# Even layer: where the modulation vectors of the experts are computed, through which slots their weights come, and when the first expert's gate is loaded

## The chip, the cores and the metric

One NeuronCore of a Trainium2 chip runs the kernel. Its engines, TensorE (PE in the rows), VectorE (DVE), ScalarE (ACT), GpSimd (POOL) and SyncE (SP, which here only issues DMAs), run their own instruction streams and meet at semaphores. The metric is the device time in microseconds of one execution.

## What is computed

A first block (gated linear recurrence beside dilated attention) makes `x` of 512 rows by 1024. Then come two layers over 512 latent and 256 context rows, the even one with a differential and a grouped attention, the odd one with a latent attention, each followed by a mixture of 16 experts. Each layer is steered by six modulation vectors, made from the condition by one wide matrix. The part that matters here is the even layer:

```python
m = silu(c) @ w_ada + b_ada          # six vectors: m[0] .. m[5], for latent and for context rows
h = modulate(rmsnorm(x), m[0], m[1])
oa = diff_attend(qa, ka, va, lam)    # the attention "ea" of the kernel
ob = gqa_attend(qb, kb, vb)          # the attention "eb"
x = x + m[2] * (concat(oa, ob) @ w_out)
h = modulate(rmsnorm(x), m[3], m[4])
aff = softmax(h @ w_router)          # then top-k tokens for each of 16 experts
y[e] = (silu(xs @ w_gate[e]) * (xs @ w_up[e])) @ w_down[e]
x = x + m[5] * scatter_add(gates * y)
```

## The kernel before

Each engine's program is written out by hand, in functions named by engine and stage (`pe_moe`, `dve_moe`, `act_norm`). An engine takes its instructions in that order, so what is written later waits behind what is written earlier.

**Weights.** SP loads all weights in one long list, `LOADS` (from line 290). Each entry has a key and a slot of 16 KB per partition; a slot is free for its next load when the matmuls of its last one are done (`slot_freed`, line 326). Slots 0 and 1 serve the projections (`two`), the experts of layer 0 cycle through `eight`. SP waits in order: a load that must wait holds up all behind it. Further waits of single loads are in `sync` (line 2882).

**Modulation vectors.** Vector j of layer l comes in two halves of 512 columns, keys `("ada", l, j, h)`, 2 MB each. `pe_ada_mm` (line 417) multiplies a half by 8 matmuls with a 32-column stationary operand, at four column positions of the array; the trace counts each matmul of this type twice. `dve_ada_row` (448) takes the result out of PSUM into a row (`row_mem`, 400). Then `pe_ada_end` (430) transposes the row into columns (j = 3, 4) or spreads it over partitions by a matmul (j = 2, 5), and `dve_ada_end` (467) puts it where it is used.

**Attentions.** `ea` (object `ATA`, line 1840) and `eb` (`ATB`, 1856) each run 48 units of 128 queries: units 0 to 31 look at 768 keys, units 32 to 47 at 256. In step s TensorE makes the scores of unit s, turns the probabilities of unit s-2 and multiplies by the values those of unit s-3. In `ea` two units are joined before the turn, so only odd units are turned. Both objects have a list of fills: extra pieces of work that each engine does when unit s-4 is through. `ea` has four small ones (copies of keys, `act_khl`, `dve_khl`), `eb` has norm pieces for VectorE and ScalarE; TensorE has none in both. The first block's attention has fills of modulation work, two matmuls at a time, from `fine` (1464).

**From attention to experts.** Behind `eb` comes the output projection (12 groups of 8 matmuls, `pe_outproj`), then `pe_moe(0)` and `dve_moe(0)`: the matmuls of vectors 3 and 4, the norm (`dve_norm`, `act_norm`), transposes and scaling (`pe_hT`, `dve_hT`), routing, top-k on VectorE, the matmuls of vector 5 under it, the indices, and the gathers of each expert's 96 rows from `h_rows` in DRAM by GpSimd. `sp_moe` (2381) writes `h_rows` and `x_rows`; it is called ahead of the second half of the first "up". The loads of vectors 3 and 4 wait for the end of `eb`, the first gate waits for the end of the output projection.

**Experts of layer 0** (`pe_experts0`): for each, gate, up and down in halves, with line 2106 for latent and 2119 for context rows.

Of the kernel before, what the change touches and what calls it, by code (L numbers as in the profile page):

```python
# [153 lines left out]
def program(nc, T, out, known):  # L154
    ctx = ExitStack()
    with ctx:
# [8 lines left out]
        AR = arena.__enter__()  # L165
# [98 lines left out]

        two, eight, ten = [0, 1], [0, 1, 2, 3, 6, 9, 4, 5], [4, 5, 0, 1, 3, 11, 9, 6, 2, 10]

# [6 lines left out]
        def expert_load(nm, l, e):  # L273
            for h in range(2):
                if (nm, l, e, h) == ("up", 0, 0, 1):
                    ada_loads(0, [5], [4, 5])
                if (nm, l, e, h) == ("gate", 1, 1, 0):
                    ada_loads(1, [5], [6, 2])
                src = T[f"w_exp_{nm}_2"][l, e, h * 512:h * 512 + 512, :]
                if (nm, l) == ("down", 0):  # L280
                    src = src.rearrange("(s p c) n -> p s (c n)", s=2, c=2)
                else:
                    src = src.rearrange("(p c) n -> p (c n)", c=4)
                cyc((nm, l, e, h), src, (4, 1024), ten if l else eight)
# [16 lines left out]
        for i, (a, b) in enumerate(EVEN_CH):  # L301
            colchunk(("even", i), T["w_in_even_2"][0], a, b, two)
        for i in range(2):
            colchunk(("oute", i), T["w_out_even_2"][0], i * 512, i * 512 + 512, two)
        ada_loads(0, [3], [8, 7])
        ada_loads(0, [4], [4, 5])
        expert_loads(0)
# [79 lines left out]
        def ada_groups(l, j):  # L387
            if l < 0:
                return [(0, 0, 128)]
            if j == 2:  # L390
                return [(1, 0, 128), (2, 1, 128)] if l == 0 else [(2, 0, 128)]
            return [(3, 0, 128), (4, 1, 128)] if l == 0 else [(3, 0, 128)]

# [6 lines left out]
        def row_mem(l, j):  # L400
            return AR[:, H0:H0 + 1024] if j == 4 else RB1

# [45 lines left out]
        def dve_ada_row(l, j, h):  # L448
            n = ADA_NO[(l, j)]
            if j == 4:  # L450
# [72 lines left out]
        def act_norm(tag):  # L523
            src, xn, nt = NORM[tag][0:3]
            for j in range(nt):
                junk = xn[:, j, :]
                if tag in ("m0", "m1"):
                    junk = AR[:, H0 + 5120:H0 + 6144]
                    S.wait_ge("res", MLAST[NORM[tag][4]], OUTP[MLAST[NORM[tag][4]]] + j)
                    if j:  # L530
                        S.wait_ge("sq", tag, j - 1)
                if tag == "no":
                    S.wait_ge(f"xr{j}", 0)
                if tag == "n1":
                    S.wait_ge(f"dx{j}", 0)
                s.activation(junk, src[:, j, :], ACT.Square, accum_out=SSQ[tag][:, j:j + 1])\
                    .then_inc(*S.up("sq", tag, j))
            act_rstd(tag)
            S.wait_ge("rs", tag)
            if tag == "m0":  # L540
                S.wait_ge("full", "ada", 0, 3, 0)
            for j in range(1, nt, 2):
                s.activation(xn[:, j, :], src[:, j, :], ACT.Copy, scale=RS[tag][1][:, j:j + 1])\
                    .then_inc(*S.up("xn_a", tag, j))
# [910 lines left out]
        units = []  # L1455
# [383 lines left out]

        ATA = Attn("ea", units, Pb4, PTb, fills={8 + 8 * i: [i] for i in range(4)})  # L1840
        units = []
        for j in range(6):
            k0, nk = (0, 768) if j < 4 else (512, 256)
            for h in range(8):
                r = h % 2
                def kready(e):
# [8 lines left out]
                                  out=OT[:, 4 + h // 2, 128 * j:128 * j + 128]))  # L1855
        ATB = Attn("eb", units, Pb4, [AR[:, H0 + 3072:H0 + 4096], GB[0], GB[3]], Rb=RbA,
                   fill=[("sq", j) for j in range(6)] + [("rstd",)] + [("mul", j) for j in range(6)])
        ssA, gsc = st(24), st(1)
# [3 lines left out]
        def pe_fillB(it):  # L1862
            pass

# [11 lines left out]
        def dve_fillB(it):  # L1876
# [5 lines left out]
            if it[0] == "rstd":  # L1882
                V.wait_ge("sub", 5)
                dve_rstd_a("sub", ssA, 1.0 / 128)
                dve_rstd_b("sub")
            if it[0] == "mul":
                j = it[1]
# [459 lines left out]
        def dve_moe(l):  # L2347
            tag = f"m{l}"
            for h in range(2):
                dve_ada_row(l, 3, h)  # L2350

            def fourth():
                for h in range(2):
                    dve_ada_row(l, 4, h)

            dve_norm(tag, fourth)
            dve_ada_end(l, 3)
            dve_ada_end(l, 4)
            dve_hT(tag)
            dve_topk(l)  # L2360
            dve_idx(l)
            dve_ada_row(l, 5, 0)
            dve_ada_row(l, 5, 1)
            dve_ada_end(l, 5)
            dve_experts1() if l else dve_experts0()

        def pe_moe(l):
            for j, b0 in ((3, 6), (4, 4)):
                for h in range(2):
                    pe_ada_mm(l, j, h, b0 + h)  # L2370
            pe_ada_end(l, 3, 6, 7)
            pe_ada_end(l, 4, 0, 1)
            pe_route(l)
            pe_topk(l)
            for h in range(2):
                pe_ada_mm(l, 5, h, 4 + h)
            pe_idx(l)
# [354 lines left out]
        def tensor():  # L2732
# [21 lines left out]
            pe_even()  # L2754
            pe_attn(ATA, lambda i: None)
            pe_pairs(ATB, pe_fillB)
# [13 lines left out]
        def vector():  # L2770
# [28 lines left out]
            V.wait_ge("full", "hturn", *HTS[-1])  # L2799
            dve_attn(ATA, dve_khl)  # L2800
            V.wait_ge("full", "pv", "ea", 47)
# [17 lines left out]
        def scalar():  # L2819
# [24 lines left out]
            S.wait_ge("full", "even", 4, 5)  # L2844
            act_attn(ATA, act_khl)
            S.wait_ge("full", "pv", "ea", 47)
# [35 lines left out]
        def sync():  # L2882
            for i, (key, src) in enumerate(LOADS):
# [9 lines left out]
                if key[0] == "ada" and key[3] == 1 and key[2] in (2, 5):  # L2893
                    sp_bias(key[1], key[2])
                if key == ("up", 0, 0, 1):
                    sp_moe(0)
                if key == ("gate", 1, 1, 1):
                    sp_moe(1)
                if key == ("ada", 1, 2, 0):
                    Q.wait_ge("scat", 0, 15)  # L2900
                    for j in range(6):
                        sp.dma_start(XALL[:, j, :], T["x_rows"][128 * j:128 * j + 128, :])\
                            .then_inc(*Q.up(f"xr{j}", 0, by=16))
                if key[0:3] in (("ada", 0, 3), ("ada", 0, 4)):
# [74 lines left out]
```

## Time and profile before

| | us |
|---|---|
| median of 3 runs | 2478.88 (2476.44 to 2479.6) |
| profiled execution, whole | 2474.44 |
| its span, first to last instruction | 2473.1 |

| engine | busy us | share of the span |
|---|---|---|
| TensorE, matmul | 2185.0 | 88% |
| TensorE, weight load | 1072.8 | 43% |
| VectorE | 904.2 | 37% |
| ScalarE | 533.9 | 22% |
| GpSimd | 254.1 | 10% |

| part of the chain that ended last | share |
|---|---|
| TensorE | 69% |
| DMA | 17% |
| VectorE | 8% |
| ScalarE | 3% |

The stages in the trace: first block to about 370 us, the even projection to 590, `ea` to 708, `eb` to 814, its output projection to 903, norm, routing and first gather to 963, the layer-0 experts to 1512, layer 1 behind them. The DMA moves next to nothing during both attentions and is busy nearly all the time from 903 us to the end of the layer-0 experts, and again in the layer-1 experts. A share of busy time is a mean over stages with different limits, so the rows further down are read stage by stage. The profiled execution is one, and is 4.4 us below the median of the three timed ones.

### The profile page before, as it was taken

The numbers are of one execution on the slowest core, as the hardware profiler recorded it, in microseconds if no ns is written. First come the engines' busy times: TensorE is split into PE (matmuls) and PEld (weight loads), VectorE is DVE, ScalarE is ACT, GpSimd is POOL, SyncE is SP. The second block draws the span as 40 slices with busy tenths as digits, with TensorE's granted clock in tenths as the row PEclk, the third lists the DMA queues.
The fourth block names the chain that finished last, engine by engine and source line by source line (L and its number), as shares of the span: only waits on it lengthen the run. The fifth ranks groups of instructions, "written<-read, shape, count | busy, mean of one in ns | idle before, by whom it ended". The sixth has DMA issues, their size and how long they took to land.

```text
span 2473.1 us, 30430 instructions
## 1 busy us (share of the span) xinstructions
PE 2185.0 (88%) x12446; PEld 1072.8 (43%) x12446; DVE 904.2 (37%) x2232; ACT 533.9 (22%) x1169; POOL 254.1 (10%) x512
## 2 busy tenths in 40 slices
PE   6998998999978996999999996889999698778776
PEld 2444544446667442444444443446665232222222
DVE  2147535526876134212222213466652511111111
ACT  2015323113555120000000002355551100000000
POOL 0000000000124110000000000132321101000000
PEclk9999999999999997999999998989999899999999
DMA  8122611101000339999999996200032799999998
GB/s 284 68 69 72 236 68 39 68 17 69 1 1 1 137 150 387 406 391 387 391 398 399 387 387 235 86 1 1 1 137 104 299 387 402 405 404 409 404 412 342
DMA packets 96680, 546.56 MB, mean 221 GB/s; under 512 B 7807, under 2 KB 10639, under 8 KB 67614
## 3 DMA queue, kind: packets, MB, share of 16 engines
q1 hardware_dynamic: 88990, 521.02, 53.3%
q0 software_dynamic: 6144, 20.98, 3.5%
q10 hardware_dynamic: 1408, 2.62, 0.3%
q8 instruction: 99, 1.62, 0.3%
q14 instruction: 39, 0.32, 0.0%
HBM read 523.62 MB, written 20.97 MB: 220 GB/s over the span
## 4 chain that ended last, share of the span: by engine, by line
PE 69%; DMA 17%; DVE 8%; ACT 3%; issue 2%; POOL 1%; SPq 1%; another core or an unknown queue 0%; ACTq 0%; DVEq 0%; POOLq 0%
PE PS L2106 14%; PE PS L1709 8%; PE PS L2119 7%; DMA AR<-in_w_exp_up_dram 6%; PE PS L981 6%; PE PS L680 5%; PE PS L2248 5%; DMA AR<-in_w_exp_gate_dram 4%; DMA AR<-in_w_exp_down_dram 4%; PE PS L691 3%; PE PS L894 3%; PE PS L1390 3%; PE PS L1224 2%; PE PS L425 2%; PE PS L715 1%
## 5 line engine op out<-in xcount | busy, mean ns | idle before, releaser
L2248 PE MATMUL PS<-AR 128*64 128x512 f32 x1536 | 359.9, 614 | 96.1 <-DMA AR<-in_w_exp_gate_dram 46.7
L2106 PE MATMUL PS<-AR 128*64 128x512 f32 x1536 | 342.9, 598 | 3.0 <-DVE AR L2174 2.0
L2248 PEld LDWEIGHTS PS<-AR 128*64 128x64 f32 x1536 | 111.1, 141 | 320.4 <-issue 251.7
L2106 PEld LDWEIGHTS PS<-AR 128*64 128x64 f32 x1536 | 106.8, 137 | 214.5 <-issue 214.4
L1709 PE MATMUL PS<-AR 128*128 128x512 f32 (+1 forms) x480 | 190.1, 552 | 0.7 <-ACT AR L616 0.7
L680 PE MATMUL PS<-AR 96*128 96x512 f32 (+3 forms) x480 | 183.3, 499 | 3.8 <-POOL AR L657 2.3
L2119 PE MATMUL PS<-AR 128*32 128x256 f32 x3072 | 181.7, 381 | 0.0
L780 DVE TENSOR_REDUCE AR<-PS 128x1 f32<-128x768 f32 (+1 forms) x160 | 135.9, 849 | 96.8 <-PE PS L680 78.4
L735 ACT ACTIVATE AR<-PS,AR 128x768 f32<-128x768 f32 (+1 forms) x160 | 130.2, 815 | 56.8 <-DVE AR L780 24.8
L691 PE MATMUL PS<-AR 128*128 128x128 f32 x800 | 118.9, 278 | 23.3 <-ACT AR L918 8.7
L981 PE MATMUL PS<-AR 128*128 128x512 f32 x320 | 137.8, 593 | 1.1 <-DVE AR L1004 0.6
L2119 PEld LDWEIGHTS PS<-AR 128*32 128x32 f32 x3072 | 91.9, 109 | 94.8 <-issue 38.9
L1709 PEld LDWEIGHTS PS<-AR 128*128 128x128 f32 x480 | 90.1, 191 | 88.3 <-issue 85.2
L691 PEld LDWEIGHTS PS<-AR 128*128 128x128 f32 x800 | 93.2, 142 | 60.0 <-issue 16.4
L680 PEld LDWEIGHTS PS<-AR 96*128 96x128 f32 (+1 forms) x480 | 82.9, 197 | 80.0 <-issue 75.1
L1390 PE MATMUL PS<-AR 128*128 128x512 f32 x256 | 111.8, 592 | 0.0
L2145 ACT COPY AR<-PS 128x512 f32<-128x512 f32 x16 | 9.4, 585 | 425.1 <-PE PS L2081 425.1
L2265 ACT COPY AR<-PS 128x512 f32<-128x512 f32 x16 | 9.4, 585 | 394.9 <-PE PS L2227 394.9
L981 PEld LDWEIGHTS PS<-AR 128*128 128x128 f32 x320 | 60.6, 190 | 77.1 <-issue 75.6
L657 POOL COPY AR<-AR 64x128 f32<-64x128 f32 x80 | 25.0, 318 | 669.3 <-ACT AR L1749 292.1
L425 PE MATMUL PS<-AR 128*32 128x512 f32 x480 | 75.3, 681 | 11.7 <-DMA AR<-in_w_ada_dram 10.4
L894 PE MATMUL PS<-AR 128*64 128x128 f32 x1216 | 80.2, 280 | 2.0 <-ACT AR L918 1.9
(345 smaller groups left out, 2446.9 us busy)
## 6 DMA issues: line engine op xcount, KB each, us to landing
AR<-in_w_exp_gate_dram SPq DMA_DIRECT2D x64, 2048.0 KB, 15.3
AR<-in_w_exp_up_dram SPq DMA_DIRECT2D x64, 2048.0 KB, 16.1
AR<-in_w_exp_down_dram SPq DMA_DIRECT2D x63, 2048.0 KB, 19.5
AR<-in_w_ada_dram SPq DMA_DIRECT2D x30, 2048.0 KB, 12.6
AR<-in_w_in_dram SPq DMA_DIRECT2D x6, 2048.0 KB, 9.1
AR<-in_w_in_even_dram SPq DMA_DIRECT2D x4, 2048.0 KB, 7.8
AR<-in_w_out_dram SPq DMA_DIRECT2D x2, 2048.0 KB, 8.0
AR<-in_w_out_even_dram SPq DMA_DIRECT2D x2, 2048.0 KB, 7.7
```

The source lines that it names most:

```text
L425: m = pe.matmul(bank(b)[c0:c0 + 32, :], (sl if l < 0 else sl2)[:, k, :], w[:, k, :], start=(k < 4), stop=(k >= 4), tile_position=(0, c0))
L680: m = pe.matmul(PS[:, p0 + a // 512, 0:e_ - a], q, u["k"][:, a:e_], start=True, stop=True)
L691: m = pe.transpose(PS[:, 4 + k // 4, 128 * (k % 4):128 * (k % 4) + 128], pc[:, 128 * k:128 * k + 128], ident)
L735: ex = s.activation(pc[:, 0:nk], pc[:, 0:nk] if A.masked else psf[:, 512 * p0:512 * p0 + nk], ACT.Exp, bias=A.mx[:, i % 8:i % 8 + 1], accu ...
L780: v.tensor_reduce(nm, sc_, AX, ALU.max, negate=True).then_inc(*V.up("mx", A.tag, i))
L894: m = pe.matmul(bank(b)[64 * r_:64 * r_ + 64, 0:128], u["v"](k), ptc[:, 128 * k:128 * k + 128], start=(k == 0), stop=(k == nn - 1), tile_p ...
L981: m = pe.matmul(bank(b), OT[:, c, 128 * j:128 * j + 128], w[:, c, :], start=(c == 0), stop=(c == 7))
L1390: m = pe.matmul(bank(b), HT4[:, k, 128 * j:128 * j + 128], w[:, k, :], start=(k == 0), stop=(k == 7))
L1709: m = pe.matmul(bank(b)[:, 0:a1 - a0], HT6[:, k, 128 * j:128 * j + 128], w[:, k, :], start=(k == 0), stop=(k == 7))
L2106: t = pe.matmul(bank(b)[64 * q_:64 * q_ + 64, :], op, w[:, c, 512 * q_:512 * q_ + 512], start=(h == 0 and c == 0), stop=(h == 1 and c == 3 ...
L2119: t = pe.matmul(bank(b + 1)[32 * q_:32 * q_ + 32, 0:256], op, w[:, c, 256 * q_:256 * q_ + 256], start=(h == 0 and c == 0), stop=(h == 1 an ...
L2248: m = pe.matmul(bank(b)[64 * q_:64 * q_ + 64, :], op, w[:, c, 512 * q_:512 * q_ + 512], start=(h == 0 and c == 0), stop=(h == 1 and c == 3 ...
```

## The change

- The six loads of vectors 3, 4 and 5 stand ahead of those of the output projection, through slots 0 and 1. They no longer wait for the end of `eb`.
- The matmuls of 3 and 4, with their row copies and ends, become fills of `ea`, from unit 30 on (steps 34 to 51), two matmuls at a time. Those of vector 5 become fills of `eb`, units 13 to 20. Its row lies in `GB[3]`, where one of its broadcasts goes as well, so that one is made last. Its end stays behind the indices.
- `eb`'s third buffer of turned probabilities moves from `GB[3]` to another place.
- `eight` begins with slots 4 and 5: the first expert's gate goes there when `eb` is done. Its "up" takes slots 0 and 1, the second gate slots 2 and 3 behind the output projection. `sp_moe(0)` is called ahead of the first "down".
- Layer 1 keeps its order.

```diff
-        two, eight, ten = [0, 1], [0, 1, 2, 3, 6, 9, 4, 5], [4, 5, 0, 1, 3, 11, 9, 6, 2, 10]
+        two, eight, ten = [0, 1], [4, 5, 0, 1, 2, 3, 6, 9], [4, 5, 0, 1, 3, 11, 9, 6, 2, 10]
...
-                if (nm, l, e, h) == ("up", 0, 0, 1):
-                    ada_loads(0, [5], [4, 5])
...
+        ada_loads(0, [3, 4, 5], two)
         for i in range(2):
             colchunk(("oute", i), T["w_out_even_2"][0], i * 512, i * 512 + 512, two)
-        ada_loads(0, [3], [8, 7])
-        ada_loads(0, [4], [4, 5])
...
-            return [(3, 0, 128), (4, 1, 128)] if l == 0 else [(3, 0, 128)]
+            return [(4, 1, 128), (3, 0, 128)] if l == 0 else [(3, 0, 128)]
...
-            return AR[:, H0:H0 + 1024] if j == 4 else RB1
+            if (l, j) == (0, 5):
+                return GB[3]
+            return AR[:, H0:H0 + 1024] if (l, j) == (1, 4) else RB1
...
-            if tag == "m0":
-                S.wait_ge("full", "ada", 0, 3, 0)
...
-        ATA = Attn("ea", units, Pb4, PTb, fills={8 + 8 * i: [i] for i in range(4)})
+        fills = {8 + 8 * i: [("khl", i)] for i in range(4)}
+        for i, it in enumerate(fine(0, 3) + fine(0, 4)):
+            fills.setdefault(30 + i * 9 // 10, []).append(it)
+        ATA = Attn("ea", units, Pb4, PTb, fills=fills)
...
-        ATB = Attn("eb", units, Pb4, [AR[:, H0 + 3072:H0 + 4096], GB[0], GB[3]], Rb=RbA,
-                   fill=[("sq", j) for j in range(6)] + [("rstd",)] + [("mul", j) for j in range(6)])
+        fillsB = [("sq", j) for j in range(6)] + [("rstd",)] + [("mul", j) for j in range(6)]
+        fillsB += [("ada", 0, 5, h, k) for h in range(2) for k in (0, 2, 4, 6)]
+        ATB = Attn("eb", units, Pb4, [AR[:, H0 + 3072:H0 + 4096], GB[0], AR[:, F0 + 14592:F0 + 15616]],
+                   Rb=RbA, fills={i: [it] for i, it in enumerate(fillsB)})
...
         def pe_fillB(it):
-            pass
+            if it[0] == "ada":
+                pe_ada_mm(0, 5, it[3], 7, it[4], it[4] + 2)
...
+            if it[0] == "ada" and it[4] == 6:
+                dve_ada_row(0, 5, it[3])
...
-                if key == ("up", 0, 0, 1):
+                if key == ("down", 0, 0, 0):
                     sp_moe(0)
...
-                if key[0:3] in (("ada", 0, 3), ("ada", 0, 4)):
-                    Q.wait_ge("full", "pv", "eb", 47)
-                if slot == 8:
-                    Q.wait_ge("full", "ot", "oute", len(ot_parts("oute")) - 1)
-                if key[0:2] in (("gate", 0), ("up", 0)):
+                if key[0:3] == ("gate", 0, 0):
+                    Q.wait_ge("read", "pv", "eb", 47)
+                if key[0:3] == ("gate", 0, 1):
                     Q.wait_ge("full", "oute", 1, 5)
```

`pe_moe` and `dve_moe` keep this work for layer 1 alone; for layer 0 they begin with the norm.

## Rows read from the trace of the kernel before

**Rows 1.** Busy time by stretch: us, PE, PEld, DVE, ACT, POOL, clock, DMA share, GB/s
```profile
260.00:290.00 30.00, 29.49 (x180) 16.33 (x179) 17.33 (x73) 9.14 (x30) 3.32 (x12) 1.00 0.61 213
...
690.00:694.00 4.00, 3.77 (x14) 2.72 (x15) 3.10 (x13) 2.40 (x9) 0.58 (x2) 0.59 0.00 0
...
1000.00:1100.00 100.00, 100.00 (x896) 41.77 (x894) 22.91 (x48) 4.67 (x12) 7.14 (x6) 1.00 1.01 393
...
1539.00:1543.00 4.00, 3.53 (x17) 3.56 (x18) 1.62 (x2) 1.49 (x3) 0.00 (x0) 0.50 1.05 387
```

**Rows 2.** The page's groups: busy us, mean ns, idle before and releaser
```profile
L2106 PE MATMUL PS<-AR 128*64 128x512 f32 x1536 | 342.9, 598 | 3.0 <-DVE AR L2174 2.0
```

**Rows 3.** Timeline of TensorE, short units of `ea`: start, us, line, idle before
```profile
681.45 0.60 PE L680 MATMUL PS<-AR 128*128 128x256 f32 x2
...
684.17 0.60 PE L680 MATMUL PS<-AR 128*128 128x256 f32 x2
684.60 0.38 PE L691 MATMUL PS<-AR 128*128 128x128 f32 x2
684.82 0.60 PE L680 MATMUL PS<-AR 128*128 128x256 f32 x2
...
695.68 0.68 PE L715 MATMUL PS<-AR 128*128 128x128 f32 x4 [0.33 <-DVE AR L817]
696.20 0.60 PE L680 MATMUL PS<-AR 128*128 128x256 f32 x2
...
707.92 2.91 PE L674 MATMUL PS<-RK,RQ 128*128 128x512 f32 x8
```

**Rows 4.** Timeline of TensorE, first block's attention with fills (line 425)
```profile
243.95 1.06 PE L425 MATMUL PS<-AR 128*32 128x512 f32 x8
244.95 0.70 PE L680 MATMUL PS<-AR 128*128 128x256 f32 x2
```

**Rows 5.** Timeline of TensorE, long units of `eb`
```profile
755.31 0.98 PE L674 MATMUL PS<-RK,RQ 128*128 128x512 f32 x4
...
756.81 0.94 PE L674 MATMUL PS<-RK,RQ 128*128 128x512 f32 x4
758.10 0.87 PE L691 MATMUL PS<-AR 128*128 128x128 f32 x6 [0.36 <-ACT AR L918]
```

**Rows 6.** Chain that ended last, in `eb`: start, us, what
```profile
757.14 0.92 ACT AR L918
```

**Rows 7.** Timeline of all engines from 903 to 956 us
```profile
903.17 7.07 PE L425 MATMUL PS<-AR 128*32 128x512 f32 x64
903.27 0.82 SPq L2936 DMA_DIRECT2D AR<-in_w_exp_gate_dram  x2
...
905.36 1.06 ACT L536 ACTIVATE AR<-AR 128x1024 f32<-128x1024 f32 x1 [5.73 <-POOL AR L1026]
...
907.49 0.16 DVE L357 TENSOR_SCALAR AR<-AR 128x6 f32<-128x6 f32 x1
...
908.97 3.23 ACT L543 ACTIVATE AR<-AR 128x1024 f32<-128x1024 f32 x3 [0.84 <-DVE AR L375]
...
912.38 1.72 PE L579 MATMUL PS<-AR 128*128 128x128 f32 x12
...
947.16 0.82 SPq L2936 DMA_DIRECT2D AR<-in_w_exp_gate_dram  x2
...
955.61 0.69 DVE L474 COPY AR<-PS 128x512 f32<-128x512 f32 x1 [0.36 <-PE PS L438]
```

**Rows 8.** Timeline of TensorE behind the layer-0 experts
```profile
1518.78 3.64 PE L425 MATMUL PS<-AR 128*32 128x512 f32 x32 [0.28 <-DVE AR L488]
...
1539.47 8.17 PE L579 MATMUL PS<-AR 128*128 128x128 f32 x48 [15.07 <-issue]
```

**Rows 9.** Chain that ended last, the first gather: start, us, what
```profile
947.81 11.73 DMA AR<-h_rows,AR
```

**Rows 10.** Landing times of the indirect writes of line 2325, min/median/max
```profile
DMA to landing us min/median/max: 4.8/9.8/12.9
```

More of the change, by code:

```diff
@@ L449, in dve_ada_row @@
             n = ADA_NO[(l, j)]
-            if j == 4:
+            if (l, j) == (1, 4):
                 res_wait(V, MLAST[l])
@@ L1838, in dve_khl, with pe_fillA, act_fillA, dve_fillA @@
                 v.tensor_tensor(a, src, hi[2].bitcast(F32), ALU.subtract).then_inc(*V.up("kl", kv, r, n))
-        ATA = Attn("ea", units, Pb4, PTb, fills={8 + 8 * i: [i] for i in range(4)})
+        fills = {8 + 8 * i: [("khl", i)] for i in range(4)}
+        for i, it in enumerate(fine(0, 3) + fine(0, 4)):
+            fills.setdefault(30 + i * 9 // 10, []).append(it)
+        ATA = Attn("ea", units, Pb4, PTb, fills=fills)
+        def pe_fillA(it):
+            if it[0] in ("ada", "ada_end"):
+                pe_fill1(it)
+        def act_fillA(it):
+            if it[0] == "khl":
+                act_khl(it[1])
+        def dve_fillA(it):
+            if it[0] == "khl":
+                dve_khl(it[1])
+            else:
+                dve_fill1(it)
         units = []
@@ L2348, in dve_moe @@
             tag = f"m{l}"
-            for h in range(2):
-                dve_ada_row(l, 3, h)
             def fourth():
@@ L2354, in fourth @@
                     dve_ada_row(l, 4, h)
-            dve_norm(tag, fourth)
-            dve_ada_end(l, 3)
-            dve_ada_end(l, 4)
+            if l:
+                for h in range(2):
+                    dve_ada_row(l, 3, h)
+                dve_norm(tag, fourth)
+                dve_ada_end(l, 3)
+                dve_ada_end(l, 4)
+            else:
+                dve_norm(tag)
             dve_hT(tag)
@@ L2361, in dve_moe @@
             dve_idx(l)
-            dve_ada_row(l, 5, 0)
-            dve_ada_row(l, 5, 1)
+            if l:
+                dve_ada_row(l, 5, 0)
+                dve_ada_row(l, 5, 1)
             dve_ada_end(l, 5)
@@ L2367, in pe_moe @@
         def pe_moe(l):
[L2368 to L2372, printed above, removed]
+            if l:
+                for j, b0 in ((3, 6), (4, 4)):
+                    for h in range(2):
+                        pe_ada_mm(l, j, h, b0 + h)
+                pe_ada_end(l, 3, 6, 7)
+                pe_ada_end(l, 4, 0, 1)
             pe_route(l)
             pe_topk(l)
-            for h in range(2):
-                pe_ada_mm(l, 5, h, 4 + h)
+            if l:
+                for h in range(2):
+                    pe_ada_mm(l, 5, h, 4 + h)
             pe_idx(l)
@@ L2754, in tensor @@
             pe_even()
-            pe_attn(ATA, lambda i: None)
+            pe_attn(ATA, pe_fillA)
             pe_pairs(ATB, pe_fillB)
@@ L2799, in vector @@
             V.wait_ge("full", "hturn", *HTS[-1])
-            dve_attn(ATA, dve_khl)
+            dve_attn(ATA, dve_fillA)
             V.wait_ge("full", "pv", "ea", 47)
@@ L2844, in scalar @@
             S.wait_ge("full", "even", 4, 5)
-            act_attn(ATA, act_khl)
+            act_attn(ATA, act_fillA)
             S.wait_ge("full", "pv", "ea", 47)
```

## The prediction

> **What bounds the kernel now.** I read the granted clock and busy table by stages first, then the page's idle column for the layer-0 experts, then the two attentions and the stretch between the output projection and the first expert. In the layer-0 experts TensorE is busy for the whole of 100 us at full clock while the DMA share is 1.01 [rows 1]; which of the two bounds it is told by the idle column: ahead of 1536 matmuls of line 2106 there are 3.0 us of idle time, put down to VectorE [rows 2]. So TensorE bounds that stage, and the saturated DMA is only its shadow. Its length (963 to 1512 us) stays, and so does what comes behind it. What the change can move is therefore three stretches, each of which passes on to the end at full value: the short units of the first attention (ATA, from 681.45 us), the second (ATB), and 903 to 963 us.
>
> **What is moved.** Three modulation vectors (j = 3, 4, 5), each two halves of 8 matmuls. Today j = 3 and 4 run behind the output projection as four halves in 7.07 us [rows 7]: all four column tiles are in use, so a half costs 1.77. In the attention they are cut into fills of two matmuls, 4 fills a half. The early attention already has such fills: one shows 1.06 us, and the next instruction starts 1.00 behind its start [rows 4]. So a half costs 4.0 there, and a fill is 1.0 us of TensorE. The Trainium skill (TensorEngine Tiling (Array Packing), Key Properties) says that tiles work in parallel and that a change of tiling mode drains the engine; the 1.00 us holds both (two tiles of four in use, two changes of mode), so nothing is added for it, and a planner who went by the full packing would reckon 1.77 where this order costs 4.0.
>
> **ATA, the short units: +6.** Sixteen fills and two ends (8 transposes each, which I take at 1.0, as another 1 us item) = 18 us go into steps 34 to 51. From 681.45 to the second attention's first matmul at 707.92 there are 26.5 us [rows 3]. TensorE's own work there, from start to start of neighbouring rows: a score 0.43, a turned pair 0.22 to 0.24, its product 0.52 [rows 3]; 14 scores, 8 turns, 8 short products and one long one (1.4) make 13.5. It idles 13. Were all of that filled, 5 us remained. Three things stand beside it. First, the clock: the granted clock is 0.59 in 690 to 694 [rows 1], and the second attention's first eight matmuls take 2.91 where two groups of four take 2 x 0.98 [rows 3, 5]; with the gaps filled I expect full clock, worth 1 us beyond the durations above. Second, the packing: with fills in it the early attention kept TensorE busy 29.49 us of 30 [rows 1], so waits nearly vanish; but here VectorE and ScalarE hand over to each other within a pair of units, and VectorE's four copies of a row (0.69 each) stand in its queue until the fill is done. Behind such a copy wait the next unit's maximum and so the exponential. I add 2 us. Third, j = 4's weights come through the two slots only when j = 3's halves are done; seven steps of about 1.8 us are there for it. Sum 5 - 1 + 2 = +6; from +4 (perfect packing) to +12 (each row copy and one weight load awaited).
>
> **ATB: +6.** Eight fills for j = 5, at steps 17 to 24, long units. The chain through a pair of units is nearly all TensorE [rows 5]: scores, turn, then ScalarE's copy of 0.92 [rows 6], under which one group of scores runs, with 0.36 idle. Four fills fall ahead of that copy and cost 1.0 each; four fall into the gap and cost 1.0 - 0.43. Together +6.3; from +5 to +8. The two VectorE additions fit its slack.
>
> **Behind the output projection: -0.5.** The last residual's square starts at 905.36 and ends 906.5, but the root starts at 907.49, behind a row copy [rows 7]; without it it starts 0.95 earlier. ScalarE's three scalings (3.23) then end at 911.25 in place of 912.2. TensorE today works through and begins the transposes at 912.38 at full clock, then waits about 1.1 in all, at first for the modulation columns. Without the matmuls TensorE is idle for 8 us, from 903.25 to 911.3. The same transposes behind a gap of 15.07 us ran at a granted clock of 0.50, the lower level of 1.2 GHz, at first [rows 1] and took 8.17 for 48 [rows 8], against 6.9 at the rate of 1.72 for 12 [rows 7]. So 0.95 + 1.1 are gained, and 1.3 to 2 of them given back. The top-k behind it is VectorE's and the same.
>
> **The gather: -5.5.** The chain shows 11.73 us for the first expert's gather of 0.39 MB [rows 9]. It shares the DMA with loads: SP's traffic starts at 903.27, and x_rows has landed at 947.16, where gate 1 and down 0 are released [rows 7], 0.7 us ahead of the gather. That is gate 0 (4.2 MB), half of up 0 (2.1), j = 5 (4.2), h_rows and x_rows (3.1 each): 16.8 MB in 43.9 us, 0.383 MB/us. After the change: half of up 0, gate 1, h_rows, x_rows, 12.6 MB = 32.9 us, landed at 936 or 937; then only down 0 (11 us more) until TensorE frees a slot. It lands at 948 or 949, against a gather at about 947.3. So the gather meets an all but empty queue. Its price there no row shows; the nearest is the indirect writes, 4.8 us at the least and 9.8 in the median [rows 10]. I take 6.2, from 4.8 to 9. A floor stands beside it: j = 5's last broadcast copy ends at 955.6 today [rows 7]; without its two row additions and its late matmuls it ends near 950.5, so no more than about 9 can be had.
> The Trainium skill (DMA: Bandwidth & Descriptors, Anatomy of one DMA) prices a DMA of this kind at 2.0 us + bytes / 436e3, an estimate of 2.9 us for the gather by that page; the sum would then reach the floor of 9 and the net would be +3 in place of +6. No run here shows such a gather.
>
> **Cost at nothing.** The layer-0 experts keep their rate, and their slots' new order still lets a load go out seven ahead of its use. At their end layer 1's first loads wait for one pair of halves later (about 11 us); the last would go out when up 15 is done, about 1499, and is used from 1518.78 [rows 8]: 20 us, cover enough. The wait on the even layer's first gate moves its load to 820 us, where the DMA is idle. SP's other move, h_rows behind up 0 and gate 1, is in the megabytes above.
>
> **Sum.** +6 + 6.3 - 0.5 - 5.5 = +6.3 us, on the profiled execution 2474.44 (span 2473.1) -> 2480.7. The median shown is 2478.88, so 4.4 above that execution; I predict against the median: 2485.
>
> **The rivals.**
> A. *Costly waits in ATA* (chance 0.17): VectorE's row copies stop the hand-over between the engines, and j = 4's loads come late: ATA +12, all else as above: 2478.9 + 12 + 6.3 - 6 = 2491. For it: VectorE is busy 3.10 of 4 us there [rows 1]. Against it: the early attention's 29.49 of 30.
> B. *A wash* (0.30): the packing is perfect (+4), and the gather needs 4.8, less 7: 4 + 6.3 - 7.5 = +2.8, or 2481.7; with ATB at +5 it is +1.5.
> C. *The other side, faster* (0.16): the layer-0 experts are in truth paced by the DMA. 12.6 MB leave the loaded time from 903 on, at 0.383 MB/us 33 us of it, and matmuls that read late data may be drawn as busy. It decides if a matmul there is longer than its columns need. If a third of it came back, -11 + 6.3: about 2474 or below. Against it: no DMA wait ahead of line 2106 [rows 2], and TensorE at full clock throughout [rows 1].
> D. *It doesn't do what it says* is small: loads still wait in order, and a late slot would give A.
> The forecast itself (+4.5 to +9, 2483.4 to 2488) has 0.37.
>
> **Chances and range.** About 0.2%, 5 us, is what a measurement of this kernel can tell from no change. Slower by more: A and nearly all of the forecast, 0.51. Within: B and the rest, 0.33. Faster by more: 0.16. As no change and slower share the weight, the likeliest case's own range stands above. For 8 in 10 the range takes in A and B and the mild end of C: 2475 to 2493.
>
> **What would show it.** Right: line 425 rows of about 1.06 us between short units from about 685 us on, the second attention's start some 6 us later at full clock, its end 12 us later; transposes of the m0 norm at a low granted clock behind an idle 8 us; a gather of 5 to 7 us; the first line-2106 matmul about 6 us later than 962.98; the layer-0 experts unchanged in length. Wrong: a gather still above 9 us (the load queue is not what made it slow), pairs in the short units still 2.9 us apart (fills are hidden), or an experts stage that is shorter than 549 us.

## The result and the profile after

| us | before | changed |
|---|---|---|
| median | 2477.85 (2474.9 to 2482.15, 16 runs) | 2485.42 (2480.52 to 2490.95, 16 runs) |
| span of the profiled execution | 2473.1 | 2483.1 |

The changed kernel takes 1.0032 of the time of the kernel before, 95% interval 1.0025 to 1.0039: slower by 8 us (the two profiled executions are 10 apart). To see where, both traces are cut at the same events. Each number below is the distance between two of them in one profiled execution.

| stretch | before | changed | difference |
|---|---|---|---|
| start to the scores of `ea`'s unit 32 | 676.66 | 678.44 | +1.8 |
| to the first scores of `eb` ("ea") | 31.26 | 38.94 | +7.7 |
| to the output projection ("eb") | 112.69 | 118.63 | +5.9 |
| to the issue of the first gather | 127.20 | 127.57 | +0.4 |
| to the first expert matmul | 15.17 | 8.01 | -7.2 |
| to the end of the layer-0 experts | 549.36 | 548.98 | -0.4 |
| to the last matmul | 947.05 | 948.99 | +1.9 |

The first line and the last hold no work of the change. The +7.7, +5.9, +0.4 and -7.2 make +6.8; the -0.4 is within what this stage differs by from kernel to kernel. Each trace is one execution, and stretches with the same code differ between executions too. In the five kernels of experiments 1, 2, 4 and 6 that keep the changed code between projection and gather, that stretch is 126.3 to 129.0, so its +0.4 is not clear of such differences.

**The first attention.** TensorE's timeline in the changed kernel (start, us, line; in brackets the idle time ahead and its releaser); L677, L688 and L712 are scores, turn and product, L424 a fill, L443 an end:

```profile
683.23 0.60 PE L677 MATMUL PS<-AR 128*128 128x256 f32 x2
...
687.04 0.70 PE L677 MATMUL PS<-AR 128*128 128x256 f32 x2
687.58 0.38 PE L688 MATMUL PS<-AR 128*128 128x128 f32 x2
687.89 1.05 PE L424 MATMUL PS<-AR 128*32 128x512 f32 x4
688.87 0.70 PE L677 MATMUL PS<-AR 128*128 128x256 f32 x2
689.41 0.61 PE L712 MATMUL PS<-AR 128*128 128x128 f32 x4
689.95 1.05 PE L424 MATMUL PS<-AR 128*32 128x512 f32 x4
690.93 0.70 PE L677 MATMUL PS<-AR 128*128 128x256 f32 x2
...
694.23 0.68 PE L712 MATMUL PS<-AR 128*128 128x128 f32 x4 [0.77 <-DVE AR L814]
...
716.33 1.20 PE L443 MATMUL PS<-AR 128*128 128x128 f32 x8 [0.24 <-DVE AR L459]
717.38 1.65 PE L671 MATMUL PS<-RK,RQ 128*128 128x512 f32 x8
```

Nearly every unit has its fill. Where two fills stand behind one unit (x8, at 686.05 and 703.63) they run as one, so the sixteen take fourteen places. A pair of units takes 3.89 us (687.04 to 690.93) where it took 2.91 in the trace of before (698.89 to 701.80):

```profile
698.89 0.60 PE L680 MATMUL PS<-AR 128*128 128x256 f32 x2
...
701.80 0.60 PE L680 MATMUL PS<-AR 128*128 128x256 f32 x2
```

Almost nothing waits. The busy table of that stretch says the same, and that the clock is now at its upper level (2.4 GHz), where before it was 0.59 for a part of it [rows 1]:

```profile
686.00:717.00 31.00, 29.64 (x153) 14.14 (x152) 19.73 (x67) 11.54 (x35) 6.08 (x17) 1.00 0.60 205
```

**The second attention.** Timeline of the changed kernel, one pair of long units with two fills:

```profile
757.54 1.53 PE L891 MATMUL PS<-AR 128*64 128x128 f32 x24
759.00 0.97 PE L671 MATMUL PS<-RK,RQ 128*128 128x512 f32 x4
759.90 1.05 PE L424 MATMUL PS<-AR 128*32 128x512 f32 x4
760.89 0.87 PE L688 MATMUL PS<-AR 128*128 128x128 f32 x6
...
761.62 0.94 PE L671 MATMUL PS<-RK,RQ 128*128 128x512 f32 x4
762.49 1.05 PE L424 MATMUL PS<-AR 128*32 128x512 f32 x4
...
764.28 1.53 PE L891 MATMUL PS<-AR 128*64 128x128 f32 x24
```

Such a pair takes 6.74 us here (757.54 to 764.28), and 5.10 without fills in the trace of before:

```profile
717.47 1.53 PE L894 MATMUL PS<-AR 128*64 128x128 f32 x24
...
722.57 1.53 PE L894 MATMUL PS<-AR 128*64 128x128 f32 x24
```

That is 1.64 for two fills. The 0.36 of waiting for ScalarE [rows 5] is gone.

**Behind the projection.** TensorE's timeline, and then a stretch of the busy table (PE, PEld, DVE, ACT, POOL, granted clock, DMA share, GB/s) of the changed kernel:

```profile
926.80 5.99 PE L576 MATMUL PS<-AR 128*128 128x128 f32 x30 [8.15 <-ACT AR L540]
932.82 1.50 PE L1952 MATMUL PS<-AR 128*32 128x512 f32 x16
```

```profile
927.00:931.00 4.00, 4.00 (x20) 3.98 (x20) 2.13 (x3) 1.21 (x3) 0.00 (x0) 0.50 1.03 434
```

TensorE idles 8.15 us and then has the lower level of its clock (1.2 GHz): the 30 transposes take 6.02 to the next instruction, where the same 30 took 4.67 before, from 912.38 [rows 7] to this line:

```profile
917.05 1.50 PE L1932 MATMUL PS<-AR 128*32 128x512 f32 x16
```

**The gather.** The timelines of SyncE, TensorE (PEld is its weight load) and GpSimd in the changed kernel, and in a second block two stretches of its busy table:

```profile
953.35 0.89 SPq L2959 DMA_DIRECT2D AR<-in_w_exp_down_dram  x2
...
962.74 5.49 PE L437 MATMUL PS<-AR 128*128 128x512 f32 x8
...
963.58 1.12 POOL L2332 DMA_INDIRECT AR<-h_rows,AR  x1 [42.26 <-DVE AR L2050]
...
967.96 1.05 PEld L2092 LDWEIGHTS PS<-AR 96*128 96x128 f32 x8 [0.55 <-DMA AR<-h_rows,AR]
968.07 1.10 PE L2092 MATMUL PS<-AR 96*128 96x96 f32 x8
971.59 3.36 PE L2126 MATMUL PS<-AR 128*64 128x512 f32 x10 [2.42 <-DVE AR L2194]
```

```profile
960.00:963.50 3.50, 0.95 (x5) 0.68 (x6) 2.84 (x11) 0.00 (x0) 0.00 (x0) 0.50 1.04 440
963.50:968.00 4.50, 4.50 (x8) 1.50 (x7) 2.73 (x7) 0.00 (x0) 2.97 (x3) 0.72 0.81 255
```

The transposes of the gathered rows begin 4.49 us behind the gather's issue, in place of 11.78 (11.73 of them for the gather [rows 9]). Their weight load waits for the gather until 967.96, 4.38 us behind the issue; the matmuls lose next to nothing by it, since TensorE comes out of vector 5's broadcasts (L437) only then. Only down 0 is in the queue, issued 10.2 us ahead of the gather. Before, gate 1 went out 0.65 us ahead of it [rows 7, 9] and down 0 0.2 us behind (948.03).

The layer-0 experts are as long as before, with the same first wait on VectorE, in the page's groups:

```profile
L2126 PE MATMUL PS<-AR 128*64 128x512 f32 x1536 | 342.6, 598 | 3.3 <-DVE AR L2194 2.4
```

### The profile page after: what moved, and what is told of

Read it like the earlier page. It is cut to its first block, busy times and chain, and to the rows that moved or that the text cites. A ratio compares the mean times of both kernels' runs of the same rounds, so it can differ in the third digit from the quotient of the medians.

```text
span 2483.1 us, 30426 instructions
## 1 busy us (share of the span) xinstructions
PE 2203.6 (89%) x12446; PEld 1078.4 (43%) x12446; DVE 904.6 (36%) x2232; ACT 534.1 (22%) x1169; POOL 253.6 (10%) x512
## 4 chain that ended last, share of the span: by engine, by line
PE 70%; DMA 15%; DVE 8%; ACT 3%; issue 2%; POOL 1%; SPq 1%; another core or an unknown queue 1%; ACTq 0%; DVEq 0%; POOLq 0%
PE PS L2126 14%; DMA AR<-in_w_exp_up_dram 8%; PE PS L1706 8%; PE PS L2139 7%; PE PS L677 5%; PE PS L978 5%; PE PS L2268 5%; DMA AR<-in_w_exp_gate_dram 4%; PE PS L688 3%; PE PS L891 3%; PE PS L1387 3%; PE PS L1221 2%; PE PS L424 2%; DMA AR<-in_w_exp_down_dram 2%; PE PS L712 1%
## 5 line engine op out<-in xcount | busy, mean ns | idle before, releaser
L2268 PE MATMUL PS<-AR 128*64 128x512 f32 x1536 | 368.9, 628 | 88.6 <-DMA AR<-in_w_exp_gate_dram 43.3
L2126 PE MATMUL PS<-AR 128*64 128x512 f32 x1536 | 342.6, 598 | 3.3 <-DVE AR L2194 2.4
L677 PE MATMUL PS<-AR 96*128 96x512 f32 (+3 forms) x480 | 184.1, 501 | 3.9 <-POOL AR L654 2.3
L688 PE MATMUL PS<-AR 128*128 128x128 f32 x800 | 118.5, 278 | 18.7 <-ACT AR L754 7.5
L677 PEld LDWEIGHTS PS<-AR 96*128 96x128 f32 (+1 forms) x480 | 82.9, 196 | 89.5 <-issue 84.7
L688 PEld LDWEIGHTS PS<-AR 128*128 128x128 f32 x800 | 93.4, 142 | 59.6 <-issue 19.3
L424 PE MATMUL PS<-AR 128*32 128x512 f32 x480 | 86.6, 674 | 11.8 <-DMA AR<-in_w_ada_dram 10.8
```

The lines of the kernel that those rows point to most:

```text
L424: m = pe.matmul(bank(b)[c0:c0 + 32, :], (sl if l < 0 else sl2)[:, k, :], w[:, k, :], start=(k < 4), stop=(k >= 4), tile_position=(0, c0))
L677: m = pe.matmul(PS[:, p0 + a // 512, 0:e_ - a], q, u["k"][:, a:e_], start=True, stop=True)
L688: m = pe.transpose(PS[:, 4 + k // 4, 128 * (k % 4):128 * (k % 4) + 128], pc[:, 128 * k:128 * k + 128], ident)
L2126: t = pe.matmul(bank(b)[64 * q_:64 * q_ + 64, :], op, w[:, c, 512 * q_:512 * q_ + 512], start=(h == 0 and c == 0), stop=(h == 1 and c == 3 ...
L2268: m = pe.matmul(bank(b)[64 * q_:64 * q_ + 64, :], op, w[:, c, 512 * q_:512 * q_ + 512], start=(h == 0 and c == 0), stop=(h == 1 and c == 3 ...
```

## The experiments

"Ea", "eb" and so on are the stretches of the table above.

**1. What the fills cost in each attention.** Two kernels leave out part of the computation: in the first, the matmuls of vectors 3 and 4 (four tiny ones a half stay, for the hand-over), in the second, those of vector 5 in the same way. Row copies, ends and loads stay.

```diff
-            if it[0] in ("ada", "ada_end"):
+            if it[0] == "ada" and it[4] == 6:
+                pe_ada_mm_last(it)         # 4 matmuls of 32 columns
+            if it[0] == "ada_end":
...
-                pe_ada_mm(0, 5, it[3], 7, it[4], it[4] + 2)
+                if it[4] == 6:
+                    pe_ada_mm_last(it, 7)
```

> Edit: in the first attention twelve of the sixteen fills issue no matmul, and the last fill of each half issues four matmuls of 32 columns; so the products of vectors 3 and 4 are left out for the most part, while VectorE's four row copies and both ends stay. Theory T: nearly all of the 7.7 us by which the first attention got longer goes, the second attention starts 6 to 8 us earlier than in the changed kernel. Rival R: the row copies keep it long, 2 us or less come back. Part of the low clock of the kernel before may return with the idle time, worth 1 to 2 us.

> Edit: in the second attention six of the eight fills issue no matmul, and the last of each half four matmuls of 32 columns (the product of vector 5 is left out for the most part); the row additions stay. Theory T: the second attention is 5 to 6 us shorter than in the changed kernel, and the start of the output projection moves by that. Rival R: 1 us or less.

Without the first sixteen, "ea" is 33.83: 5.1 of the 7.7 us come back, where 6 to 8 were expected. What is left for the other 2.6 are the two ends, the four tiny fills (0.2 each) and VectorE's row copies; this run does not tell them apart, and in it some units had the low clock, as before. Timed once, 2479.99 us. Without the last eight, "eb" is 113.40 against 118.63, 5.2 less. This understates them: in that execution the last turns of `eb` had the low clock. From the first to the last scores of `eb` the two traces show 107.80 and 101.16, so the eight fills cost 6.6. Timed once, 2479.7 us.

**2. Four matmuls a fill.** All fills with four matmuls in place of two, so half as many.

```diff
-                pe_ada_mm(0, 5, it[3], 7, it[4], it[4] + 2)
+                pe_ada_mm(0, 5, it[3], 7, it[4], it[4] + 4)
```

> Edit: each fill of modulation work in the two even attentions makes four matmuls (all four column tiles) in place of two, so there are half as many fills; same result, same VectorE row copies. Theory T (the attentions pay for TensorE time, and a fill costs about 1.0 us whether it fills two tiles or four): the fills of the first attention shrink from 16 to 8 us and fit its idle 13 us, so the second attention starts 5 to 7 us earlier than in the changed kernel (there 7.7 us behind the kernel before), the second attention gains 2.5 to 3 us; whole time 2476 to 2479, 7 to 10 us below the changed kernel. Rival R (the price is VectorE's row copies, which stand in its queue until a fill is done, and the order they force): the copies are all there, so no more than 2 us come back, 2483 to 2486.

Timeline of TensorE with four a fill (the trace counts each matmul twice):

```profile
685.36 1.06 PE L424 MATMUL PS<-AR 128*32 128x512 f32 x8
686.36 0.70 PE L677 MATMUL PS<-AR 128*128 128x256 f32 x2
```

A fill of twice the work costs the same 1.0 us. The Trainium skill (TensorEngine Tiling (Array Packing), Key Properties) has tiles at different positions work in parallel; by that rule the price of a fill is its longest column of tiles, and the trace agrees: 1.00 to the next start at four positions, 0.98 at two. "Ea" falls by 2.8 us to 36.18, where 5 to 7 were expected, and "eb" to 116.25. Three rounds: 2479.32 us, 1.0007 of the kernel before (0.9997 to 1.0016), so 6 us of the 8 are gone. The fills are thus the larger part of the price, but not all of it: eight fills and two ends still cost 4.9 us in "ea", although a pair of units had 1.3 us of idle time before.

**3. Vector 5 back behind the projection, and the fills spread out.** In the first kernel vector 5 goes to where vectors 3 and 4 were before, and its loads go out at the end of `eb`; the second also has fills of four matmuls in `ea`, one for every second unit.

```diff
-        fillsB += [("ada", 0, 5, h, k) for h in range(2) for k in (0, 2, 4, 6)]
...
+            else:
+                for h in range(2):
+                    pe_ada_mm(0, 5, h, 6 + h)
...
+        for i, it in zip((30, 32, 34, 36, 38, 40, 42, 44, 46, 47), fineq):
```

> Edit to the changed kernel: vector 5 is taken out of the second attention; its weights are loaded at the attention's end into the two places that held vector 3's, and its two halves run behind the output projection, four tiles at a time, where TensorE stood idle for 8 us; its row additions sit between the norm's steps. The first attention keeps its fills of two. Theory T: the second attention is back at its length of the kernel before (112.7 us from its first matmul to the projection's, in place of 118.6), and the matmuls cost nothing behind the projection. If the low clock of the transposes came from the idle 8 us, they now start at full clock and the stretch from projection to gather falls by 1 to 2 us. Sum 6 to 8 us below the changed kernel: 2477.5 to 2480. Rival: the matmuls or row additions delay the norm, and 2 to 3 us of it are lost there again: 2481 to 2482.

> Edit: as the run with vector 5 behind the projection, and the first attention's fills make four matmuls each and stand one in each pair of units (units 30, 32, ... 46) in place of four in a row. Theory T, as the run with four to a fill left it (fills in a row make TensorE the bound of these units, 2.9 us a pair becomes 3.9; one fill a pair, 1.6 + 1.0 = 2.6 us, fits under the hand-over between VectorE and ScalarE): the first attention is 1 to 3 us longer than in the kernel before (that had 31.3 us from unit 32's scores to the next attention), the second as long; with the 7 us that the stretch behind the projection gave, 2472 to 2475, below both kernels. Rival R (what is left over, 2.6 us with empty fills, grows with VectorE's part wherever the fills stand): the first attention stays 5 us longer, 2476 to 2478.

The first: "eb" 111.93, and the stretch to the gather 127.47, as before. Vector 5's 3.64 us of matmuls lie in TensorE's idle 8 us and cost nothing, where in `eb` they cost 6.6. The clock did not come back, as had been expected: 4.59 us of idle time are left behind them, and the transposes have the low clock again (a granted clock of 0.50 from 919 to 921) and take 5.92 to the next instruction, at 925.01:

```profile
919.09 5.78 PE L579 MATMUL PS<-AR 128*128 128x128 f32 x30 [4.59 <-ACT AR L543]
```

2477.18 us, 1.0002 (0.9988 to 1.0015). The second did not bring what was expected in "ea", 1 to 3 us more than before: it stays at 38.26. A typical pair takes 3.31 us (684.61 to 687.92), with idle time left in it. The chain that ended last shows why:

```profile
692.05 1.00 PE PS L425 x8
693.05 0.64 PE PS L680 x2
693.71 0.42 DVE AR L780
...
695.78 0.48 DVE AR L804
696.27 0.20 DVE AR L825
696.47 0.65 DVE AR L460
697.11 0.33 DVE AR L780
```

The fill (L425) stands directly ahead of the scores (L680) for which VectorE's maximum (L780) waits. Those scores come just in time, so this fill lies on the chain in full, however much TensorE idles elsewhere in the pair. From 683 to 714 us five of the eight fills are on the chain (5.0 us). Where a fill is not, the chain runs through VectorE and ScalarE alone, as from 693.71 to 697.11. All four of VectorE's row copies (L460) are on it, 2.6 us in all. The two together are 7.6, near the 7.0 by which this "ea" is longer than before. 2475.75 us, 0.9994 (0.9983 to 1.0005).

**4. The row copies on ScalarE.**

```diff
+            if it[0] == "ada" and it[4] == 6:
+                l, j, h = it[1:4]
...
+                s.copy(row_mem(l, j)[:, 512 * h:512 * h + 512], bank(S.bank_of(("ada", l, j, h))))\
...
-            else:
+            elif it[0] == "ada_end":
```

> Changed kernel with the four row copies of vectors 3 and 4 in the first attention on ScalarE in place of VectorE. With empty fills 2.6 of the 7.7 us of that stretch remained, which left the copies (4 times 0.65) and the two ends. If VectorE's queue is what the copies lengthen, the stretch from the scores of unit 32 to the second attention falls from 38.94 to 36.4 to 37.4. Rival: any engine of the hand-over is as good as another, ScalarE's exponential waits behind the copy in the same way, and the stretch stays at 38.5 to 39.5.

"Ea" is 38.23 (678.14 to 716.37), between the two expectations: 0.7 us, a quarter of what four copies take. With a fill behind nearly every unit TensorE is the bound, and little is left for VectorE's queue to add; with spread fills, as the chain above has it, the copies weigh more. Timed once, 2480.74 us.

**5. The low clock behind the projection.** 32 useless matmuls (7.07 us) in TensorE's idle time.

```diff
+                for n in range(32):
+                    c0 = 32 * (n % 4)
+                    pe.matmul(bank(7)[c0:c0 + 32, :], sl2[:, n % 8, :], w[:, n % 4, 0:512], start=True, stop=True,
+                              tile_position=(0, c0))
```

> Changed kernel with 32 further matmuls (a useless product, about 7 us) in TensorE's 8.15 us of idle time behind the output projection; the sum of those for vectors 3 and 4 that the kernel before had there. If the low granted clock of the transposes costs what the 1.0 us of scaling and the removed wait gained (1.3 to 2 us, the prediction's step), the first transposes run at full clock and the stretch from the projection's first matmul to the gather falls from 127.6 to 126 or 126.3. Rival: the stretch is paced by VectorE and ScalarE and the clock of the transposes is hidden: it stays at 127.3 to 127.8, with a granted clock near 1.00 in it.

Busy table of this kernel over the transposes, and then its timelines of TensorE and SyncE:

```profile
924.70:930.70 6.00, 5.64 (x46) 4.22 (x46) 3.87 (x5) 2.82 (x5) 0.00 (x0) 1.00 1.01 427
```

```profile
916.45 7.07 PE L2404 MATMUL PS<-AR 128*32 128x512 f32 x64
924.68 1.69 PE L576 MATMUL PS<-AR 128*128 128x128 f32 x12 [1.16 <-ACT AR L540]
...
951.59 0.89 SPq L2968 DMA_DIRECT2D AR<-in_w_exp_down_dram  x2
...
966.15 1.20 PE L2092 MATMUL PS<-AR 96*128 96x96 f32 x8 [1.20 <-DMA AR<-h_rows,AR]
```

The clock stays at its upper level, and the stretch to the gather falls to 126.17: the low clock costs 1.4 us in these two executions. The same transposes behind the same 8.15 us took 5.23 in the kernel of experiment 2 and 6.21 in that of experiment 4, so the cost is not the same each time. But none of the 1.4 arrives. The gather, issued 8.5 us behind down 0 (960.06 behind 951.59) in place of 10.2, takes 6.1 us in place of 4.4. By experiment 6 that is because it meets more of that load. Timed once, 2482.25 us.

**6. What makes the gather slow.** Down 0 of the changed kernel is held until the indices are known, so that it goes out with the gather. Then, in the kernel before, the loads from gate 1 on are held until the gather has landed.

```diff
                 if key == ("down", 0, 0, 0):
                     sp_moe(0)
+                    idx_wait(Q, 0)
```

```diff
+                if key == ("gate", 0, 1, 0):
+                    Q.wait_ge("gath0", 0, 0)
```

> Edit: the first down weights (4.2 MB) are not issued at the landing of x_rows but when the indices are there, that is at the same time as the first gather; nothing else. Theory Q (the gather was slow before since it shared the DMA with loads): the gather takes 8 to 11 us again and the first expert's matmuls start 4 to 6 us later than in the changed kernel. Rival: the gather's time does not hang on the loads (order of the queues, or the write of h_rows just ahead, made it slow), and it stays at 4 to 5 us with a start within 1 us.

> Edit to the kernel before: the second gate's and the first down's loads (8.4 MB), which it issues 0.7 us ahead of the first gather, wait until that gather has landed; all else stays. Theory Q (the loads that share the DMA make the gather slow): the gather takes 6 to 8 us in place of 11.73 (half of the first up is still landing), the first expert starts 3 to 4 us earlier, bounded by the broadcast copies that end at 956.3; no stall later since the held loads are needed only from 977 us on: 2474 to 2476. Rival: the held loads come late and TensorE waits for them in the first expert: no gain or a loss.

With down 0 issued 0.26 us ahead of the gather, the chain reads:

```profile
966.33 9.60 DMA AR<-h_rows,AR
```

The time from the gather's issue to the first expert grows by 5.2 us, so a load put beside the gather is enough to make it slow. The whole, timed once, is 2493.37 us (2478.76 before on the same chip). That is more than the 5.2: in this execution the output projection took 84.75 us in place of 82.64, and the last turns of `eb` had the low clock. In the other kernel the gather has landed after 7.6 us, when the held load goes out, and nothing waits for it. But TensorE comes to the transposes only 8.45 us behind its issue (950.64), out of vector 5's broadcasts, each of which waits for VectorE's copy of the one before:

```profile
952.74 6.52 PE L438 MATMUL PS<-AR 128*128 128x512 f32 x8 [2.87 <-DVE AR L458]
958.26 1.13 SPq L2938 DMA_DIRECT2D AR<-in_w_exp_gate_dram  x2
959.09 1.09 PE L2072 MATMUL PS<-AR 96*128 96x96 f32 x8
```

2475.57 us, 0.9983 of the kernel before (0.9972 to 0.9993): this one wait is already a gain.

**7. The broadcast copies away.** In the changed kernel with vector 5 behind the projection and spread fills, the broadcasts run under the top-k, with their copies on ScalarE.

```diff
+            if l == 0:
+                for gi, si, np_ in ada_groups(0, 5):
+                    for h in range(2):
+                        S.wait_ge("full", "adab", 0, 5, gi, h)
+                        s.copy(GB[gi][0:np_, 512 * h:512 * h + 512], bank(S.bank_of(("adab", 0, 5, gi, h)))[0:np_, :])\
```

> Edit: as the run before it, and vector 5's broadcast (four matmuls, four copies) stands under the top-k, with the copies on ScalarE, which is idle there, in place of behind the indices. Theory F (in the changed kernel the first expert waits not for the gather but for those copies on VectorE, which end at 968.96 while the gather has landed by 968): the first expert's scaling starts right behind its transposes, 0.5 to 1 us earlier than without the edit; no more, since the gather then ends last. If the gather had landed long before, up to 3 us.

No gain, where 0.5 to 1 us was expected: 4.53 us from gather to transposes, as with the copies on VectorE (4.49). In the changed kernel gather and copies end nearly together, and the gather alone needs its 4.4 to 4.5. 2480.37 us, 1.0004 (0.9995 to 1.0014). That median is 4.6 us above the one of the kernel with spread fills, on which this one is built (6.2 between the profiled executions). Yet from the scores of unit 32 to the first expert the two traces differ by 0.1 (286.06 and 285.96). The rest is in code that the two share: 2.7 us ahead of unit 32, 0.6 in the layer-0 experts and 2.8 behind them.

**8. The gain without its price.** The kernel before, with both attentions as they were. Its loads from the second half of up 0 on are held until the gather has landed, and vector 5's rows and broadcasts go to ScalarE, under the top-k. One more thing differs: the first half of gate 0 (2.1 MB) no longer waits for the output projection and goes out during it.

```diff
-                if key[0:2] in (("gate", 0), ("up", 0)):
+                if key == ("up", 0, 0, 1):
+                    Q.wait_ge("gath0", 0, 0)
+                if key[0:2] in (("gate", 0), ("up", 0)) and key != ("gate", 0, 0, 0):
...
+            if l == 0:
+                act_ada5()
```

> Kernel before, with its attentions untouched; the loads from the second half of up 0 on held until the first gather has landed, and vector 5's row and broadcast copies made by ScalarE under the top-k (the bias added by an accumulating matmul). The two attentions should be the 31.3 and 113 to 114 us of the kernel before. If the gather's price is the loads beside it, and the next limit is the row of copies on VectorE (the run that held the loads alone stopped at 8.45 us from gather to transposes with VectorE's copies ending there), the gather's stretch falls from 11.78 to about 4.5 us and the first expert starts 7 us earlier: about 2471.5 to 2473, ratio 0.996 to 0.998 to the kernel before. Rival 1: the copies are no limit, the stretch stays at 8 to 8.5 and the time that of the run that held the loads alone (2475.6, ratio 0.9983). Rival 2: the held loads come late for up 0 and down 0, the first experts wait for weights and the stage is more than 551.5 us long: 2475 or above.

GpSimd's, SyncE's and TensorE's timelines:

```profile
865.08 41.55 SPq L2963 DMA_DIRECT2D AR<-in_w_exp_gate_dram  x2
...
950.39 1.12 POOL L2318 DMA_INDIRECT AR<-h_rows,AR  x1 [41.46 <-DVE AR L2036]
...
954.73 0.35 SPq L2963 DMA_DIRECT2D AR<-in_w_exp_up_dram  x1
...
954.76 1.56 PE L2078 MATMUL PS<-AR 96*128 96x96 f32 x8 [5.13 <-DMA AR<-h_rows,AR]
...
958.36 5.34 PE L2112 MATMUL PS<-AR 128*64 128x512 f32 x16 [2.05 <-DVE AR L2180]
```

The gather lands in 4.34 us (SP's next load, which waits for it, goes out at 954.73; none went out since 925) and the first expert matmul comes 7.97 us behind its issue, in place of 15.17. "Ea" is 31.30 and "eb" 114.29, the latter longer than before only by turns at the low clock at its end. The experts take 548.98: the held loads are not missed. Five rounds: 2471.17 us against 2478.55, 0.9973 (0.9962 to 0.9983). This kernel beats both. What the earlier half of gate 0 adds to it was not run by itself.

## Why the prediction was right

It gave 2485 us, from a sum of +6.3. The sum by the table is +6.8, and the median 2485.42. The mechanism was right: fills that are paid in full in both attentions, against a gather that no longer meets loads. That the number fits so closely is luck in part. Two terms were off by some 1.7 us each, with opposite signs. And the 2485 stood on a median of 2478.88 from three executions, where sixteen give 2477.85; the measured difference of the medians is 7.6.

**`ea`, +6: measured +7.7.** The form of the sum holds, its terms do not. From 683.23 to 717.38 are 34.15 us. Fills and ends are 15.8 of them and not 18, since two pairs of fills run as one (fourteen places of 0.98 to 1.00, and ends of 0.96 and 1.05). The waits, 0.71 + 0.77 + 0.35 + 0.24, are 2.1. That leaves 16.3 for the attention's own work, where the sum had 13.5. This is the term that was mis-sized: beside a fill, scores take 0.54 from start to start and a turned pair 0.31, and not the 0.43 and 0.24 of [rows 3]. So the "+2 for packing" stands for 2.8 of longer neighbours and 2.1 of waits, less 2.2 of fills. The "-1 for the clock" was booked in the wrong stretch: the sum of `ea` was made of durations at full clock already, and what the clock bought was the first eight matmuls of `eb`, 1.65 in place of 2.91 [rows 3], of which 0.7 reaches the next matmuls (3.07 in place of 3.77 from start to start). And the row copies, for which rival A stood, were worth 0.7. The price of a fill was read from a row of four matmuls, not two: [rows 4] has x8, and the trace counts each twice. It holds for two as well, as experiment 2 shows, but the same row already said that a fill of four costs no more. j = 4's weights did not come late: no fill of this stretch waits for a DMA.

**`eb`, +6.3: measured 6.6** for the fills (5.9 with the faster start). Two fills a pair cost 1.64 against 1.0 + 0.57.

**Behind the projection, -0.5: measured +0.4.** The 0.95 from the row copy is there: from the projection's start to the first transpose it is 90.79 us in place of 91.77. The low clock costs 1.4, inside the 1.3 to 2 given. The step that failed is the 1.1 of waits: from the first transpose to the gather it is 35.37 with the clock held up and no modulation matmuls, and 35.43 before. TensorE's waits in it, put down to VectorE's scaling (line 600, 603 before), are the same 0.4 and 0.75 in the trace of before and in that of experiment 5, so they were never waits for the modulation columns.

**Gather, -5.5: measured -7.2.** Right in cause. The size was wrong by the price of an undisturbed gather: 6.2 taken, 4.3 to 4.5 measured; the lower bound of 4.8 from [rows 10] was nearer. The floor of 9 set beside it was mis-sized: the last broadcast copy starts at 955.61 [rows 7], and ends 0.69 later, and in the changed kernel the last copy ends 5.4 us behind the gather's issue (968.97), not the 3 of the prediction. So copies and gather bound this stretch together, and about 7 us was all that could be had. With the same code behind the indices, but the broadcasts at the low clock (6.57 us in place of 5.49), it came out at 9.07 in the kernel of experiment 2, 1.1 longer. The time of the load behind it was also off: down 0 went out at 953.35, and 936 to 937 moved by the 12 us of the attentions is 948 to 949. The gather still met its tail (share 1.04 up to 963.5) and lost nothing by it. The Trainium skill's estimate of 2.9 us (DMA: Bandwidth & Descriptors, Anatomy of one DMA) is short of the 4.34 measured with no load beside it; here the measurement decides.

**The experts as long as before: right.** Rival C (they are paced by the DMA) wanted 11 us out of that stage; it moved by 0.4. In all kernels measured it lies between 547.1 and 550.1, with loads early or late.

What would have been cheaper was not seen: the 8 us in which TensorE idles behind the projection are free for vector 5 (experiment 3), and the gain of the change needs no matmul in an attention (experiment 8). Open is the +1.8 ahead of the change and the +1.9 in layer 1. Stretches with unchanged code shift by so much between executions. The first line of the table is 675.92 to 678.68 in all thirteen traces, and at the end of `eb`, four turns of six matmuls took 0.87 each before, and in experiment 8 three of the four took 1.5.

## What to carry to other kernels

Idle time of an engine is room for other work only at the point of a step where nobody waits just in time for its next instruction. Before filling a gap inside a loop, look for a gap outside of it, and let a fill use all column positions, since half a fill costs as much. Ahead of a small transfer that everything waits for, hold the large loads back: a wait of one line did more than a rearranged schedule.

## What the runs showed of the hardware

- The price of a gather of 96 rows (0.39 MB) goes by what was queued ahead of it. From issue to landing: 4.3 us with no load issued for 25 us, 4.4 with one pair of 2 MB loads issued 10.2 us earlier, 6.1 with 8.5 us earlier, 9.6 with 0.3 us earlier, and 11.7 with one pair issued 0.65 us earlier and another 0.2 us later.
- A fill of four 128*32 matmuls at four column positions and one of two at two positions take the same 1.0 us, and the neighbour in the full-array form is 0.1 us longer beside it.
- After 8.15 and 4.59 us of idle TensorE the granted clock was 0.50, after 1.16 us it was 1.00; the same 30 transposes took 6.02, 5.92 and 4.62 us to the next instruction.
